# Two stages of a Trainium2 kernel rearranged: the recurrence's products first, the triangular inverse solved beside the convolution's

## The reference, cut to what matters

```python
hn = _rmsnorm(h_res, norm_in_g[l]); P = hn @ w_in[l]       # 2048 x (4*1024 + 128 + 4*1024)
Pr = Pr + (prev - Pr) * mu_shift[l]                        # r, k, v, g_r, two LoRA inputs
w_raw = -softplus(-(w0 + tanh(wl) @ w_lora_up)) - 0.5; decay = exp(-exp(w_raw))
a = sigmoid(a0 + al @ a_lora_up)
kk = (k*k_k) / max(norm(k*k_k), 1e-12); k = k * (1 + (a - 1) * k_a)
# recurrence per head (16 heads of 64): S_t = S_{t-1} diag(w_t) - (S_{t-1} kk_t)(kk_t a_t)^T + v_t k_t^T ; y_t = S_t r_t
y_a = (groupnorm(y)*lnx_g + lnx_b + sum(r*k*r_k)*v) * silu(g_r)
y_b = Bg * causal_conv3(Cg * hc) * silu(g_c)
h_res = h_res + concat(y_a, y_b) @ w_out
```

## Time and profile before

| | us |
|---|---|
| median of 3 runs | 2693.23 (2691.91 to 2694.07) |
| profiled execution, its own time | 2697.28 |
| its span, first to last instruction | 2695.6 |
| PE busy | 2569.9 (95%) |
| DVE busy | 1827.6 (68%) |
| ACT busy | 1303.0 (48%) |
| POOL busy | 344.7 (13%) |

### The profile page before, as it was taken

The page is one execution under the profiler, slowest core; times in us unless marked ns, Lnnn a source line. Parts: engine busy times, 40 slices in busy tenths (PEclk is TensorE's granted clock), DMA queues, the critical chain, the costliest instruction groups (busy, mean ns, idle before and its releaser), DMA issues.

```text
span 2695.6 us, 43718 instructions
## 1 busy us (share of the span) xinstructions
PE 2569.9 (95%) x15162; PEld 2255.4 (84%) x15162; DVE 1827.6 (68%) x2630; ACT 1303.0 (48%) x2054; POOL 344.7 (13%) x375
## 2 busy tenths in 40 slices
PE   6999998587999999999999999999999999999997
PEld 6999995486878888888888888788888888888886
DVE  6888886646866666665666667676666756666665
ACT  5455456454545444544444445645445444444544
POOL 3112114512220000000000000110000101000012
PEclk8999999898999999999999999999999999999998
DMA  6666660005756666666666666567667766667673
GB/s 185 178 173 171 179 170 18 12 7 141 206 162 176 178 187 178 176 181 186 179 182 178 178 189 162 155 175 184 186 178 191 177 192 183 175 180 193 178 180 94
DMA packets 757373, 441.72 MB, mean 164 GB/s; under 512 B 28305, under 2 KB 720529, under 8 KB 757297
## 3 DMA queue, kind: packets, MB, share of 16 engines
q1 hardware_dynamic: 752016, 430.16, 57.3%
q0 software_dynamic: 5280, 10.56, 3.0%
HBM read 437.35 MB, written 3.31 MB: 163 GB/s over the span
## 4 chain that ended last, share of the span: by engine, by line
PE 72%; DVE 2%; ACT 1%; issue 0%; DMA 0%; DVEq 0%; POOL 0%; SPq 0%; ACTq 0%; POOLq 0%
PE bank L271 37%; PE bank L273 19%; PE bank L295 4%; PE bank L296 4%; PE bank L297 4%; PE bank L1522 1%; PE bank L1541 1%; PE bank L1529 1%; DVE lob L238 1%; PE bank L1542 1%; PE bank L1521 1%; ACT xx L1694 1%; DVE xx L1860 0%; DVE x L1877 0%; DVE x L1875 0%
## 5 line engine op out<-in xcount | busy, mean ns | idle before, releaser
L271 PE MATMUL bank<-xx,hib 128*128 128x512 f32 x3328 | 1202.0, 404 | 10.6 <-DVE lob L238 10.6
L238 DVE TENSOR_TENSOR lob<-rawb,hib 128x1024 fp32r<-128x1024 f32 x672 | 825.3, 1240 | 395.1 <-ACT hib L231 388.8
L231 ACT ACTIVATE hib<-rawb 128x1024 fp32r<-128x1024 f32 x672 | 699.6, 1055 | 524.3 <-PE bank L273 363.6
L273 PE MATMUL bank<-xx,lob 128*128 128x256 f32 x3328 | 937.0, 282 | 0.0
L271 PEld LDWEIGHTS bank<-xx,hib 128*128 128x128 f32 x3328 | 627.5, 189 | 159.7 <-DVE lob L238 11.3
L273 PEld LDWEIGHTS bank<-xx,lob 128*128 128x128 f32 x3328 | 631.4, 190 | 1.4
L271 PE MATMUL bank<-oo,hib 128*128 128x512 f32 x1024 | 356.9, 393 | 14.5 <-DVE gT L1794 12.8
L254 PE MATMUL bank<-xh,hia 128*128 128x258 f32 (+2 forms) x1040 | 301.0, 289 | 12.2 <-DVE xl L413 12.2
L255 PE MATMUL bank<-xl,hia 128*128 128x258 f32 (+2 forms) x1040 | 297.4, 286 | 0.0
L256 PE MATMUL bank<-xh,loa 128*128 128x258 f32 (+2 forms) x1040 | 296.5, 285 | 0.0
L273 PE MATMUL bank<-oo,lob 128*128 128x256 f32 x1024 | 287.2, 281 | 0.0
(11 more groups left out here) (303 smaller groups left out, 2615.0 us busy)
## 6 DMA issues: line engine op xcount, KB each, us to landing
rawb<-in_a_w_in_dram SPq DMA_DIRECT2D x256, 512.0 KB, 4.6
rawa<-in_w_in_dram SPq DMA_DIRECT2D x130, 512.0 KB, 5.0
rawb<-in_kv_w_dram SPq DMA_DIRECT2D x128, 512.0 KB, 4.6
rawb<-in_b_w_in_dram SPq DMA_DIRECT2D x128, 512.0 KB, 5.2
rawb<-in_a_w_out_dram SPq DMA_DIRECT2D x64, 512.0 KB, 5.2
rawb<-in_b_w_out_dram SPq DMA_DIRECT2D x64, 512.0 KB, 5.1
rawb<-in_w_out_dram SPq DMA_DIRECT2D x32, 512.0 KB, 5.4
table<-in_rel_dram POOLq DMA_DIRECT2D x32, 128.0 KB, 4.0
```

The lines of the kernel that those rows point to most:

```text
L231: nc.scalar.activation(self.hi[(2 * at.u + h) % SPL][:], self.raw[at.u % RAW][:, h * HALF:(h + 1) * HALF], ACT.Copy).then_inc(hi_ready, 1)
L238: nc.vector.tensor_tensor(self.lo[b][:], self.raw[at.u % RAW][:, h * HALF:(h + 1) * HALF], self.hi[b][:].bitcast(F32), ALU.subtract).then_ ...
L271: nc.tensor.matmul(out, self.hi[b][:, w], both(k).rearrange("p a t -> p (a t)"), start=start and k == 0, stop=False)
L273: last = nc.tensor.matmul(out[:, 0:SEQ], self.lo[b][:, w], both(k)[:, 0], start=False, stop=stop and k == 7)
```

## The change

The order of stage one becomes: all recurrence units first (eight tiles of k, r, v, g, `row_unit`), then all convolution units (eight tiles of four, `conv_unit`), every loop written out. What the order makes possible is moved:

- **The `aab` products** (`within`) are made in stage one, one group a tile, in the second half of the next tile's first unit: 3 token groups x 2 heads, each a product of 64 rows, heads on rows 0 to 63 and 64 to 127 into different PSUM banks, with no spreading. DVE masks them (`keep_within`, two operations of 96x288), SP stores them (`keep_aab`, six transfers a tile of 32-float pieces) before the second load of a tile.
- **The inverse** is solved by DVE in pieces (`solve_beside`) after the split of each half from the fourth unit of the second convolution tile on: 16 pieces half by half, then one in every three halves, seven of them. A step's product is now three operations, one for each block, in place of one of four dimensions. The result is stored at the end of stage one's block.
- **Stage two is gone.** `ark` moves to the start of stage three, behind the transposes: six products of 64 rows for each of 24 pairs, into two alternating pairs of banks; of three pairs DVE evacuates and masks two in one operation a head, ACT copies the third and POOL masks it.
- **Sigmoids** are made from tanh (ACT) and a scale and shift, in place of exp, add and reciprocal; the convolution's gate is finished on POOL.
- **Slots**: stage one's stream has three raw slots, the second stream four. The gates read the LoRA weights directly, and parameters are read where they lie.

```diff
-    FIRST = [0, META - 2, 0, META - 2, META - 2, META - 2, META, META]
+    FIRST = [0, META - 2, 0, META - 2]
+    FIRST_CONV = [META - 2, META - 2, META, META]
-        st = Stream(ph, "a")
+        st = Stream(ph, "a", 3, 0)
@@ SP
+                def keep_aab(i):
+                    sp.wait_ge(aab_taken, 2 * (i + 1))
+                    dst = aab_d.rearrange("(t c) (p e) s u -> c p e s t u", c=TC, e=2)
+                    for c in range(TC):
+                        w = slice(C * c, C * c + C)
+                        for e in range(2):
+                            sp.dma_start(dst[c, i, e], aab[w, NT * e:NT * e + NT, w]).then_inc(aab_out, 16)
+                for i in range(CT):
+                    for n in range(4):
+                        if n == 1 and i >= 2:
+                            keep_aab(i - 2)
+                        st.load_columns(sp, row_unit(i, n), w_in, ...)
@@ PE
+                def within(i):
+                    def emit():
+                        pe.wait_ge(kap_made, i + 1)
+                        wait(pe, aab_taken, 2 * i)
+                        for n in range(NT):
+                            w = slice(TT * n, TT * n + TT)
+                            for e in range(2):
+                                r = slice(64 * e, 64 * e + 64)
+                                mm = nc.tensor.matmul(psum[6 + e][0:TT, w], bk[r, i, 0, w], kr[r, i, 0, w], start=True,
+                                                      stop=True)
+                                if n == NT - 1:
+                                    mm.then_inc(aab_sum, 1)
+                    return emit
+                for i in range(CT):
+                    st.unit(pe, row_unit(i, 0), L, xh, xl, ({4: gates(i)}, {2: within(i - 1)} if i else {}), FIRST[0])
+                    st.unit(pe, row_unit(i, 1), L, xh, xl, ({}, {}), FIRST[1])
+                    st.unit(pe, row_unit(i, 2), L, xh, xl, ({2: key_norm(i)}, {}), FIRST[2])
+                    st.unit(pe, row_unit(i, 3), L, xh, xl, ({2: bonus(i)}, {}), FIRST[3])
+                for i in range(CT):
+                    for n in range(4):
+                        st.unit(pe, conv_unit(i, n), L, xh, xl, ({}, {2: within(CT - 1)} if (i, n) == (0, 0) else {}),
+                                FIRST_CONV[n])
@@ POOL, the convolution's gate
+                    ch.link(g.tensor_scalar(egc[:], egc[:], 0.5, 0.5, ALU.mult, ALU.add))
+                    ch.link(g.tensor_tensor(egc[:], egc[:], pgc[:], ALU.mult))
...
+                    g.tensor_tensor(yb[:, i], egc[:], cv[:], ALU.mult).then_inc(yb_made, 1)
@@ ACT
+                    a(t["ez"][:, 0:L], psum[2][:, 0:L], ACT.Tanh, bias=half[:, i, 0:1], scale=0.5).then_inc(z_used, 1)
@@ DVE
+                def keep_within(i):
+                    wait(dve, aab_out, 32 * TC * i)
+                    dve.wait_ge(aab_sum, 2 * i + 2)
+                    for e in range(2):
+                        tt(aab[:, NT * e:NT * e + NT], psum[6 + e][0:TT, 0:LP].rearrange("p (a t) -> p a t", a=NT),
+                           mask[:, 0:1].broadcast_to([TT, NT, TT]), ALU.mult).then_inc(aab_taken, 1)
+                def solve(s):
...
+                    if s < H2 - 1:
+                        n = s + 1
+                        for b in range(3):
+                            ch(tt(prod[:, b, 0:n, 0:n], block_of(sx, b, 0, (C, n), (1, n)), block_of(sa, b, n, (0, n), (C, n)),
+                                  ALU.mult))
+                        ch.settle()
+                        ch.link(v.tensor_reduce(blocks(sx, n, (C, n)), prod[:, :, 0:n, 0:n], AX_X, ALU.add))
...
+                def solve_beside(at, h):
+                    n = 2 * (at.u - SYS_FROM) + h
+                    if 0 <= n < H2:
+                        solve(n)
+                    elif n >= H2 and (n - H2) % 3 == 0:
+                        solve(H2 + (n - H2) // 3)
@@ stage three, PE
+                    if i == 0:
+                        for n in range(PAIRS):
+                            u, p = divmod(n, CT)
+                            if n >= 2 and (n - 2) % 3 == 2:
+                                pe.wait_ge(ark_act, act_pairs(n - 2))
+                            elif n >= 2:
+                                pe.wait_ge(ark_dve, dve_pairs(n - 2))
+                            s = slice(TT * u, TT * u + TT)
+                            for kind, (left, right) in enumerate(((0, 1), (1, 0), (1, 1))):
+                                for e in range(2):
+                                    r = slice(64 * e, 64 * e + 64)
+                                    mm = mmul(psum[4 + 2 * (n % 2) + e][0:TT, TT * kind:TT * kind + TT], bk[r, p, left, s],
+                                              kr[r, p, right, s], start=True, stop=True)
+                                    if kind == 2:
+                                        mm.then_inc(ark_sum, 1)
+                    pe.wait_ge(ark_pool, 2 * act_pairs(PAIRS - 1))
@@ stage three, DVE
+                    for e in range(2):
+                        ins = tt(ark[:, u, 2 * p + e], psum[4 + 2 * (n % 2) + e][0:TT, 0:3 * TT].rearrange(
+                            "p (k t) -> p k t", k=3), mask[:, 1:4], ALU.mult)
+                    ins.then_inc(ark_dve, 1)
```

More of the change, by code:

```diff
@@ L56 @@
 HALF = 8 * P
-RAW = 4
 SPL = 4
@@ L205, in _build, with __init__ @@
     class Stream:
[L206 to L207 removed]
+        def __init__(self, stack, tag, slots, first):
+            self.slots, self.first = slots, first
+            self.raw = [sbuf(stack, f"raw{tag}{i}", [P, 2 * HALF]) for i in range(slots)]
+            self.raw_in = [sem(f"raw_in_{tag}{i}") for i in range(slots)]
             self.hi = [sbuf(stack, f"hi{tag}{i}", [P, HALF], F32R) for i in range(SPL)]
@@ L474, in split_ahead, with carve @@
-        def split_ahead(step, at, h, last):
-            j = 2 * at.u + h + AHEAD
-            if not (last and j >= 2 * U_WOUT):
-                step(At(j // 2, at.loops), j % 2)
-        with nc.Block() as block:
-            @block.sync
+        half = sbuf(ph, "half", [P, CT, 2])
+        uu = sbuf(ph, "uu", [P, SEQ + 2])
+        cv, pgc, egc = (sbuf(ph, n, [P, SEQ]) for n in ("cv", "pgc", "egc"))
+        AREA = 8704
+        area = sbuf(ph, "area", [P, AREA])
+        used = [0]
+        def carve(n, at=None):
+            if at is None:
+                at, used[0] = used[0], used[0] + n
+            assert at + n <= AREA
+            return area[:, at:at + n]
@@ new lines, in _ @@
+                for i in range(CT):
+                    split_ahead(hi, conv_unit(i, 0), 0)
+                    if i == 0:
+                        gate(CT - 1)
+                    split_ahead(hi, conv_unit(i, 0), 1)
+                    q = conv_unit(i, 0)
+                    computed(act, q)
+                    if i > 0:
+                        conv = conv_unit(i - 1, 2)
+                        act.wait_ge(taken[conv.bank()], conv.evacuated())
+                    a(uu[:], GB[q.bank()][:, META - 2:L], ACT.Copy).then_inc(taken[q.bank()], 1)
+                    for n in range(1, 4):
+                        for h in range(2):
+                            split_ahead(hi, conv_unit(i, n), h)
+                    q = conv_unit(i, 3)
+                    computed(act, q)
+                    wait(act, yb_made, i)
+                    a(pgc[:], GB[q.bank()][:, META:L], ACT.Copy).then_inc(conv_gate, 1)
+                    a(egc[:], GB[q.bank()][:, META:L], ACT.Tanh, scale=0.5).then_inc(taken[q.bank()], 1)
@@ L984, in _ @@
                         m = TC * i + c
+                        if m == 1:
+                            for n in range(2, PAIRS, 3):
+                                u, p = divmod(n, CT)
+                                pool.wait_ge(ark_act, act_pairs(n))
+                                for e in range(2):
+                                    v = ark[:, u, 2 * p + e]
+                                    g.tensor_tensor(v, v, mask[:, 1:4], ALU.mult).then_inc(ark_pool, 1)
                         wait(pool, bkt_ready, 2 * (m - 1))
```

631 lines of the change are left out of this document (286 added, 345 removed).

## The result

The changed kernel takes 2647.52 us, the median of four runs (2640.09 to 2649.66), against 2693.65 us for the kernel before beside it (2691.91 to 2696.05): a ratio of 0.9823, 95% interval 0.9802 to 0.9844. The forecast was 2652 us. The profiled execution took 2648.6 us, its span is 2647.0 us, 48.6 less than before.

The account below looks back on a forecast made before the run. PE was taken to bound stage one, a 77.6 us chain, mostly DVE operations and DRAM trips, the border. -73.2 + 23.6 + 8.0 + 1.0 - 0.3 = -40.9 gave 2656.4, less 4.05 for the median 2652 us; 8 in 10: 2636 to 2674.

Parts of the forecast that it names:

- what would show it: Signs: first transpose near 438 us, PE gapless to about 433, groups 0.7 us, ark pairs every 0.98, inverse steps 0.1 to 0.5.
- The border: Between stage one and the recurrence: the 77.6 us stretch goes, a 4.4 us tail replaces it, -73.2 us.
- Ark: Before the recurrence on PE: 24 pairs at 0.98 us, paced by two pairs of banks, +23.6 us (16 to 30).
- Groups in stage one: Products for the inverse moved onto a full PE: eight groups at 1.0 us each, +8.0 us (5 to 13).
- DVE in the recurrence's tiles: Stage one's recurrence units: DVE's work falls from 42.3 to 34.2 us a tile, hidden by PE's own work, cost 0.
- The solve beside the convolution: 36 us of DVE work on the inverse fits 45 us of room among convolution units, +1 us (0 to 31).
- Small: Gate weights' copy goes, -0.3 us; with three slots a load may take 8.9 us and landed in 5.0; half clock stays.
- (a): Rival: DVE is overrun by the inverse beside the convolution, PE loses 31 us in place of 1, 2682 us; chance 0.12.
- (b): Rival: PE's row halves don't run side by side, +5 us in ark and +4 in groups, 2661 us; chance 0.15.
- (d): Rival: the reorder doesn't shorten the border, POOL's tail or a wait for the inverse stays, 10 us more, 2662; chance 0.04.
- (c): Rival: loads pace stage one, slower than before from landings of 10.9 us, 2707 us at 11.5; chance 0.04.

Follow-up runs that it names:

- experiment 1: Changed kernel with each of the eight groups of products for the inverse in stage one issued twice into the same banks: 2650.27 us.
- experiment 10: Changed kernel with both heads' instructions reading rows 0 to 63, in stage one's groups and in ark: 2655.87 us.
- experiment 3: Changed kernel with the inverse solved in one go after DVE's last work of stage one, not between the convolution's units: 2680.41 us.
- experiment 6: Changed kernel with a solve step's product as one four-dimensional operation again, not three: 2646.19 us.
- experiment 4: Changed kernel with the last seven pieces of the inverse behind seven halves in a row, not one in three halves: 2657.88 us.
- experiment 5: Changed kernel with two raw slots in place of three in stage one's stream: 2653.83 us.
- experiment 2: Changed kernel with all instructions of head 0 (rows 0 to 63) before those of head 1, in stage one's groups and in ark: 2648.98 us.
- 8: Changed kernel with four pairs of banks in turn for ark, not two: 2641.91 us.
- experiment 9: Changed kernel with four pairs of banks for ark, both heads of a pair taken by one instruction, and one four-dimensional product a solve step: 2637.76 us.
- 7: Changed kernel with 28 PE products that nobody reads behind stage one's last: 2651.89 us.
- 11: Kernel of experiment 9 with 28 PE products that nobody reads put behind stage one: 2642.91 us.

## Why the prediction was right, point by point

The forecast was 4.5 us above the measured median and 7.8 above the profiled execution's own time; all five signs of "what would show it" came out but for sizes (the first transpose at 434.27 us, not near 438; ark pairs every 0.83 us, not 0.98). The parts' errors don't cancel: each of the first three and the fifth came out a little cheaper than forecast, and the start of stage one too. That the median was met more closely than the profiled execution is luck: I took off 4.05 us for the difference between the two before, and after the change it was 1.1 us.

1. **The border** (-73.2): measured -73.8. The tail is as described. POOL's scale took 0.41 us and its two products 0.72 each, where I had taken 0.92 for all three from a row of another stage; from POOL's end to the first transpose it is 0.55 us, where I had allowed 0.6.
2. **Ark** (+23.6): measured +20.2, the term that was furthest off. A ring of two pairs that alternates between PE and the evacuation was right, and so was its end, DVE or ACT. Mis-sized were the products, 0.50 us a pair in place of 0.72, and the evacuation, where one operation takes the 0.45 us that I had, but the two of a pair overlap and take 0.82 us, not 0.90. With these, and my 0.25 and 0.1 as they were, the same formula gives (0.50 + 0.25 + 0.82 + 0.1)/2 = 0.84 us a pair; the trace has 0.83 at full clock. The first error is in the reading of the earlier trace rows: I took what the gate products saved as a factor inside the run. Experiments 1 and 10 separate the two: inside it is two (0.085 us for two instructions or for one), and going to 64 rows and back costs 0.36 us outside. Against this stands 1.7 us of transposes at half clock, which the earlier trace rows had too.
3. **Groups in stage one** (+8.0): measured 8 x 0.88 = 7.0. The products are cheaper than I had them, 0.52 us in place of 0.72, and the two changes of mode dearer: 0.36 us by experiment 1, where I had 0.28 with the drain.
4. **DVE in the recurrence's tiles** (0): PE is busy for 185.00 of 185.00 us from 60 to 245 us, with DVE at 153.45. What the tanh form of the sigmoids is worth isn't shown: no run put exp and reciprocal back.
5. **The solve beside the convolution** (+1): measured 0.25 us. Its 37.8 us (experiment 3) were forecast as 36, steps without the wait for POOL included (experiment 6). The margin was thin: what the spacing of the last pieces saves is 10 us (experiment 4).
6. **Small** (-0.3): here stage one gave back more than I had forecast. The sum of 3 and 5 is +7.3, the mark says +5.3, and the 2.0 us between them lie at the start, where the third unit begins 2.4 us sooner (45.17 in place of 47.54 us): the first gate products come 0.85 us sooner, and the first tile of before has a stretch at half clock behind an idle PE that the change doesn't have. The window 40 to 46 us of the kernel before and of the changed one:

```profile
40.00:46.00 6.00, 5.28 (x28) 4.95 (x29) 1.64 (x2) 3.42 (x6) 0.00 (x0) 0.72 0.38 108
```
```profile
40.00:46.00 6.00, 6.00 (x47) 5.64 (x48) 4.49 (x8) 3.29 (x6) 0.00 (x0) 1.00 0.47 134
```

   Which edit of the first tile did this wasn't tried, and this start varies by 1.3 us among kernels that share its code.

Of the rivals, (a) is refuted by the step rows and by experiment 6, (b) by experiment 10, which costs the 8 to 9 us that (b) had said (+5 and +4), (d) by the 3.72 us. (c) did not happen, and its threshold was too near: experiment 5 shows that the loads have several us more room than part 6 gave them.

## What to carry to other kernels

A serial solve on an element-wise engine behind a barrier can go into the slack of a stage that another engine bounds, if it is cut into pieces no longer than the lag that the buffers allow; here its 38 us cost PE 0.25 us. Done at the end they made the kernel 33 us longer, and with the last pieces too close together ten. Small products of 64 rows belong together in one long run with their row halves alternating, and the run needs enough banks in turn that its evacuation isn't in series with it: four pairs in place of two brought the 24 pairs from 20 to 12.5 us. A duration read off an operation whose end coincides with another engine's may be that engine's and not its own; look for the coincidence before replacing the operation.

## What the runs showed that I had not expected

- **Instructions on the two row halves overlap even when the program gives all of one half first** (experiment 2: starts 4 to 6 ns apart, +1.4 us in ark where serial halves cost 5.07).
- **The half clock at the start of the recurrence comes and goes.** After the same 3.4 us of an idle PE the granted clock over the transposes is 0.50 to 0.56 in the changed kernel and in experiments 2, 4, 5, 6 and 10, and 1.00 in 1, 8 and 9. It was worth 1.7 us of transposes here and up to 2.5 with the first pairs. What decides it is open, and the dummy products of 7 and 11 don't prove that they prevent it. In 2 and 10 a second such stretch follows behind the mark (0.64 from 467.5 to 472.3 us in 10): there the sixteen products with the inverse take 4.55 us, not 2.87.
- **28 products in one place came with 3 to 5 us more far behind it**, in both kernels (from `w_out` on 2052.8 us against the change's 2048.0, and 2053.5 against experiment 9's 2050.7), and with four waits of 0.6 to 1.3 us that no semaphore explains. The waits are in no other trace. The longer stretch is less certain: other kernels without the products reach 2051.5 us.
- **Two raw slots were nearly enough** (8.55 us of 400, none of them between 49 and 337 us), with ACT waiting 136 us for loads and PE 4.3 us for DVE.
